# Output projection of a streaming encoder layer: the first norm in two vector steps, and the order of the vector and scalar engines' work around it

## The reference

```
mix = concat([y_a, y_b], -1) @ w_out
x = layer_norm(ALPHA * x + (1 + g1) * mix, ln1_g, ln1_b)
h = layer_norm(x) * (1 + sc2) + sh2
gate, up = split(h @ w_ffn_up, 2)
ffn = (silu(gate) * up) @ w_ffn_down
x = layer_norm(ALPHA * x + (1 + g2) * ffn, ln2_g, ln2_b)
```

## Time and profile before

| | |
|---|---|
| median of 3 runs | 1773.69 us (1767.19, 1773.69, 1774.83) |
| profiled execution, own time | 1767.71 us |
| its span | 1766.1 us |
| busy in the span | PE 1568.9 (89%), DVE 909.8 (52%), ACT 490.5 (28%), POOL 407.5 (23%) |
| mean granted clock of PE | 0.95 of full |

### The profile page before, as it was taken

One profiled execution on the slowest core, in us unless ns is written; L12 is line 12 of the kernel. 1 busy time (PEld: TensorE's weight loads), 2 busy tenths in 40 slices (PEclk: granted clock), 3 DMA queues, 4 the chain that ended last, 5 costly groups with the idle time before them and its releaser, 6 DMA issues.

```text
span 1766.1 us, 25689 instructions
## 1 busy us (share of the span) xinstructions
PE 1568.9 (89%) x9409; PEld 1435.9 (81%) x9409; DVE 909.8 (52%) x1511; ACT 490.5 (28%) x1169; POOL 407.5 (23%) x563
## 2 busy tenths in 40 slices
PE   5897898989886799848879899999999999999994
PEld 3797898979776699737659798998989989899882
DVE  5425566443464467525662545355363462644658
ACT  4531333343443355323443120211202112011110
POOL 4888876600221122113430000000000000000012
PEclk9898999999898899869989999999999999999997
DMA  9221333333333422182115210201202112011112
GB/s 319 74 82 50 97 96 88 105 120 96 114 72 73 123 95 91 7 140 82 71 54 174 71 61 23 59 24 47 71 12 59 42 29 71 23 49 48 28 44 79
DMA packets 139037, 135.25 MB, mean 77 GB/s; under 512 B 14289, under 2 KB 113105, under 8 KB 138961
## 3 DMA queue, kind: packets, MB, share of 16 engines
q1 hardware_dynamic: 135760, 121.48, 24.7%
q10 hardware_dynamic: 2880, 11.72, 1.6%
q0 software_dynamic: 320, 1.05, 0.2%
HBM read 109.54 MB, written 23.51 MB: 75 GB/s over the span
## 4 chain that ended last, share of the span: by engine, by line
PE 43%; DVE 3%; issue 2%; POOL 1%; DMA 1%; ACT 0%; POOLq 0%; DVEq 0%; ACTq 0%; SPq 0%
PE bank L233 29%; PE bank L1681 14%; DMA wraw<-w_up 1%; DVE dtmp L1758 1%; DVE acc L1814 1%; POOL xt L1572 0%; DVE stat L1826 0%; DVE acc L1762 0%; DVE stat L1512 0%; ACT hp L1472 0%; DVE wlo L223 0%; DVE xt L1533 0%; ACT whi L218 0%; POOL rstd L1557 0%; DVE otmp L1530 0%
## 5 line engine op out<-in xcount | busy, mean ns | idle before, releaser
L233 PE MATMUL bank<-hT_hi,whi 128*128 128x384 f32 x1512 | 496.7, 329 | 19.6 <-DVE wlo L223 15.5
L233 PE MATMUL bank<-hT_hi,wlo 128*128 128x384 f32 x1512 | 495.1, 327 | 0.0
L233 PE MATMUL bank<-hT_lo,whi 128*128 128x384 f32 x1512 | 494.8, 327 | 0.0
L233 PEld LDWEIGHTS bank<-hT_hi,whi 128*128 128x128 f32 x1512 | 285.7, 189 | 22.3 <-issue 11.9
L233 PEld LDWEIGHTS bank<-hT_lo,whi 128*128 128x128 f32 x1512 | 285.8, 189 | 0.5
L233 PEld LDWEIGHTS bank<-hT_hi,wlo 128*128 128x128 f32 x1512 | 285.5, 189 | 0.0
L1758 DVE TENSOR_TENSOR dtmp<-bank,g2r 128x512 f32<-128x512 f32 (+1 forms) x198 | 135.3, 686 | 132.6 <-PE bank L1681 132.6
L1663 POOL TENSOR_SCALAR rstd<-stat 128x1 f32<-128x1 f32 (+1 forms) x9 | 11.8, 1313 | 767.6 <-DVE stat L1830 767.6
L1681 PE MATMUL bank<-wd_hi,hid_hi 128*128 128x512 f32 (+1 forms) x396 | 160.4, 405 | 13.7 <-DVE dtmp L1758 13.7
L223 DVE TENSOR_TENSOR wlo<-wraw,whi 128x1024 fp32r<-128x1024 f32 (+1 forms) x73 | 88.8, 1219 | 144.2 <-ACT whi L218 143.9
L1681 PE MATMUL bank<-wd_lo,hid_hi 128*128 128x512 f32 (+1 forms) x396 | 156.4, 395 | 0.0
(11 more groups left out here) (360 smaller groups left out, 2582.9 us busy)
## 6 DMA issues: line engine op xcount, KB each, us to landing
wada<-w_ada SPq DMA_DIRECT2D x12, 2048.0 KB, 14.2
wraw<-w_up SPq DMA_DIRECT2D x44, 512.0 KB, 3.8
wraw<-w_down SPq DMA_DIRECT2D x22, 512.0 KB, 3.5
wraw<-w_in SPq DMA_DIRECT2D x21, 512.0 KB, 4.2
rows<-convrow ACTq DMA_DIRECT2D x16, 577.5 KB, 3.0
stg<-rows SPq DMA_DIRECT2D x9, 768.0 KB, 4.7
xall<-x_prompt SPq DMA_DIRECT2D x8, 512.0 KB, 6.6
wraw<-w_out SPq DMA_DIRECT2D x8, 512.0 KB, 4.1
```

Source lines behind the costliest of these rows:

```text
L233: last = nc.tensor.matmul(ps[banks[c]][:, 0:cw], w[:, slot, k * P:(k + 1) * P], a[:, k, c0:c0 + cw], start=(k == 0 and n == 0), stop=(k == ...
```

## The change

The norm's first application no longer goes through ACT and POOL. DVE itself computes (x - mean) * weight in one instruction and, once POOL has the reciprocal root, * rstd + bias in a second. POOL loses -mean*rstd of the first norm and the addition over the whole tile; ACT loses its first normalising pass. The remainder `wlo` of tile t+2 is made directly behind the first of the two steps, in front of the work on tile t-2. ACT's rounding of `whi` for tile t+2 goes ahead of `modulate`, and ACT, not DVE, rounds the modulated rows to `hT_hi`, behind `modulate`.

```
--- before.py
+++ after.py
@@ -64,7 +64,7 @@
 
 COUNTED_ON = {
     "o_T": ("g_T", 3 * TILES), "wo_mm": ("g_row", TILES), "f_dn": ("g_kv", TILES * HEADS),
-    "ms_hi": ("g_n", 2 * TILES), "o_n1": ("g_kdec", TILES), "o_n2": ("g_E", 3 * TILES), "h2_mod": ("g_so", TILES),
+    "ms_hi": ("g_n", 2 * TILES), "o_n2": ("g_E", 3 * TILES), "h2_mod": ("g_so", TILES),
     "f_hi": ("g_Vb", TILES * HEADS),
     "ms_lo": ("g_mix", TILES), "o_tmp": ("g_S", TILES * HEADS), "o_r": ("g_X", TILES * HEADS * LV), "o_bn": ("g_A", TILES * HEADS),
     "o_mv": ("g_QK", TILES), "o_xg": ("g_qd", TILES), "h2_hi": ("g_Xm", 2 * TILES), "h2_lo": ("g_X0", 2 * TILES),
@@ -1472,6 +1472,8 @@
                     last = act.activation(hp2[:, k, 0:n], ps[6 + k // 4][:, (k % 4) * P:(k % 4) * P + n], ACT.Identity,
                                           scale=onep[:, 1, k, tok:tok + 1], bias=modc[:, 6 + k // 4, k % 4, tok:tok + 1])
                 last.then_inc(on["h2_mod"], 1)
+                act.wait_ge(on["h2_mod"], alone(act, since("h2_mod", u + 1)))
+                act.activation(hT_hi[:, :, tile_cols(u)], hp2[:, :, 0:n], ACT.Copy).then_inc(on["h2_hi"], 1)
 
             def step(t, s):
                 n = tile_rows(t)
@@ -1479,13 +1481,10 @@
                     for j in range(2):
                         act.wait_ge(on["wo_mm"], since("wo_mm", PTILES + j))
                         ffn_hi(act, 0, j)
+                if not (isinstance(t, int) and t > PTILES - 2):
+                    tile_hi(act, t + 2, s)
                 if not (isinstance(t, int) and t < 2):
                     modulate(t - 2)
-                if not (isinstance(t, int) and t > PTILES - 2):
-                    tile_hi(act, t + 2, s)
-                act.wait_ge(on["o_rs"], since("o_rs", t * 2 + 1))
-                act.wait_ge(on["o_bn"], since("o_bn", t * 4 + 2))
-                normalise(act, xt[0:n, s, :], xt[0:n, s, :], n, 0, on["o_n1"])
                 act.wait_ge(on["o_rs"], since("o_rs", t * 2 + 2))
                 act.wait_ge(on["x1_ready"], since("x1_ready", t + 1))
                 act.wait_ge(on["o_T"], since("o_T", t - 1))
@@ -1515,8 +1514,6 @@
 
             def split_h2(u):
                 n = tile_rows(u)
-                dve.wait_ge(on["h2_mod"], since("h2_mod", u + 1))
-                dve.tensor_copy(hT_hi[:, :, tile_cols(u)], hp2[:, :, 0:n]).then_inc(on["h2_hi"], 1)
                 dve.wait_ge(on["h2_hi"], since("h2_hi", u + 1))
                 dve.tensor_tensor(hT_lo[:, :, tile_cols(u)], hp2[:, :, 0:n], hT_hi[:, :, tile_cols(u)].bitcast(F32), ALU.subtract).then_inc(on["h2_lo"], 1)
 
@@ -1537,14 +1534,19 @@
                     for j in range(2):
                         ffn_lo(dve, 0, j)
                 stats(xt[0:n, s, :], n, 0, t * 4 + 2, on["o_mv"])
+                dve.wait_ge(on["ln1_rows"], 32)
+                dve.wait_ge(on["o_mv"], alone(dve, since("o_mv", t * 2 + 1)))
+                dve.scalar_tensor_tensor(out=xt[0:n, s, :], in0=xt[0:n, s, :], scalar=stat[0:n, 0, 12:13], in1=ln1r[0:n, 0, :],
+                                         op0=ALU.subtract, op1=ALU.mult).then_inc(on["o_xg"], 1)
+                if not (isinstance(t, int) and t > PTILES - 2):
+                    tile_lo(dve, t + 2, s)
                 if not (isinstance(t, int) and t < 2):
                     split_h2(t - 2)
-                dve.wait_ge(on["o_n1"], since("o_n1", t + 1))
-                dve.wait_ge(on["ln1_rows"], 32)
-                dve.tensor_tensor(xt[0:n, s, :], xt[0:n, s, :], ln1r[0:n, 0, :], ALU.mult).then_inc(on["o_xg"], 1)
-                if not (isinstance(t, int) and t > PTILES - 2):
-                    tile_lo(dve, t + 2, s)
-                dve.wait_ge(on["x1_ready"], since("x1_ready", t + 1))
+                dve.wait_ge(on["o_rs"], since("o_rs", t * 2 + 1))
+                dve.wait_ge(on["o_xg"], alone(dve, since("o_xg", t + 1)))
+                dve.scalar_tensor_tensor(out=xt[0:n, s, :], in0=xt[0:n, s, :], scalar=rstd[0:n, 0, 0:1], in1=ln1r[0:n, 1, :],
+                                         op0=ALU.mult, op1=ALU.add).then_inc(on["x1_ready"], 1)
+                dve.wait_ge(on["x1_ready"], alone(dve, since("x1_ready", t + 1)))
                 stats(xt[0:n, s, :], n, 1, t * 4 + 4, on["o_mv"])
 
             wo_steps(dve, step)
@@ -1564,12 +1566,11 @@
 
             def step(t, s):
                 n = tile_rows(t)
-                g = Steps(pool, on["o_p"], since("o_p", t * 4))
+                g = Steps(pool, on["o_p"], since("o_p", t * 3))
                 pool.wait_ge(on["o_mv"], alone(pool, since("o_mv", t * 2 + 1)))
-                pool.wait_ge(on["o_n1"], alone(pool, since("o_n1", t)))
-                rstd_steps(pool, g, n, 0, LN_EPS, on["o_rs"])
-                pool.wait_ge(on["o_xg"], alone(pool, since("o_xg", t + 1)))
-                pool.tensor_tensor(xt[0:n, s, :], xt[0:n, s, :], ln1r[0:n, 1, :], ALU.add).then_inc(on["x1_ready"], 1)
+                pool.wait_ge(on["x1_ready"], alone(pool, since("x1_ready", t)))
+                g(pool.tensor_scalar(rstd[0:n, 0, 0:1], stat[0:n, 0, 13:14], LN_EPS, None, ALU.add))
+                pool.tensor_tensor(rstd[0:n, 0, 0:1], rstd[0:n, 0, 0:1], mhalf[0:n, 0:1], ALU.pow).then_inc(on["o_rs"], 1)
                 pool.wait_ge(on["o_mv"], alone(pool, since("o_mv", t * 2 + 2)))
                 pool.wait_ge(on["o_n2"], alone(pool, since("o_n2", t)))
                 rstd_steps(pool, g, n, 1, LN_EPS, on["o_rs"])
```

## The result

| | before | changed |
|---|---|---|
| median, runs of one chip | 1770.87 us (4 runs, 1767.19 to 1774.83) | 1751.53 us (4 runs, 1748.4 to 1753.5) |
| ratio | | 0.9891, 95% interval 0.9868 to 0.9913 |
| span of the profiled execution | 1766.1 us | 1750.0 us |
| PE busy | 1568.9 | 1570.8 |
| DVE / ACT / POOL busy | 909.8 / 490.5 / 407.5 | 919.0 / 488.6 / 387.6 |

What follows compares the result with a forecast made beforehand. A ring of waits through ACT, DVE and POOL was taken to keep PE idle in the output projection. 13.8 + 5.7 + 1.3 - 0.3 = 20.5 us off the 1770.9 mean gives 1750.4 us, range 1744 to 1756.

Steps and rivals of the forecast that it cites:

- The five gaps: Output projection, tiles 4 to 8: PE's five waits for wlo, 10.7 us, all go; tile 8 ends 13.8 us earlier.
- The slack of `wlo`: Output projection: wlo now needs only whi, so DVE can lag by 6 us before PE idles once.
- The ring that stays: Output projection: one turn through ACT, DVE, POOL takes 12.0 us, 13.0 with POOL held; DVE 0.5 late at tile 8.
- POOL under back-to-back vector work: First norm: POOL's two small operations beside DVE's vector instructions cost 0.1 us a tile, between 0 and 1.08.
- Rival 3: Output projection: POOL shut out by three vector instructions, turn 15.1 us, 4.6 us slower, 1775.5 us; chance 0.02.
- Start of the FFN: Behind tile 8: PE's gap before the first FFN weights shrinks from 9.08 to 3.4 us, gaining 5.7 us.
- Clock: First FFN block, 48 matmuls: PE's clock may stay high after the 3.4 us gap, gain 1.3 us, bounds 0 and 2.7.
- Last tile: Before the last hT_lo: ACT rounds at half width instead of DVE's cast, costing 0.3 us.
- Behind it: After the last hT_lo: the next pair's FFN weight loads move along with PE and ACT, costed at nothing.
- Rival 2: Behind the last hT_lo: gain given back by later loads or clock, gain 8 to 14 us, 1757 to 1763; chance 0.08.
- rival 4: In the tiles: PE still waits, whi behind a late xn; 5.4 us gain left, 1765.5 us; chance 0.04.
- Rival 1: Output projection: turn of 13.0 us with POOL held, DVE 4.5 late at tile 8, gain 14.6, 1756 us; chance 0.24.

Runs made afterwards that it cites:

- the two part-alone runs: The changed kernel's norm alone, order and engines of before, ratio 0.9888; the kernel before with whi and wlo early and ACT rounding hT_hi, ratio 1.001.
- the run with the late `hT_lo`: The changed kernel with hT_lo of tile t-2 moved behind the second statistics; ratio to the kernel before 0.9859.
- the early weight: The changed kernel with the first FFN weight split in tile 7's step, a tile earlier; ratio to the kernel before 0.986.
- the filler: The changed kernel with 26 unused matmuls on PE between tile 6's transposes and the first FFN block; ratio to the kernel before 0.9907.

## Why the prediction was right, point by point

*What bounds.* Right: the ring through ACT, DVE and POOL held PE, and the two part-alone runs show it from both sides. The one turn that the prediction read, 15.18, is near the loop's others (14.09, 15.36), but the unrolled tiles ran at 12.96 and 12.51 already.

*The five gaps.* Right. Forecast 13.8 us, measured 13.65 (822.37 to 906.83 is 84.46; 823.79 to 894.60 is 70.81).

*The slack of `wlo`.* True but idle: I gave the moved `wlo` credit for the gaps ("so DVE can lag by 6 us before PE idles once"). With `wlo` back behind `hT_lo` no gap came back either. That order was good enough once the ring was short.

*The ring that stays.* The turn was right (12.0, or 13.0 where POOL is held; measured 12.24, 13.21, 13.31 in the loop). What failed is the step after it, "I take 0.5" for the lag, since at PE's pace DVE would start each tile after a short wait. That holds up to tile 4. But a turn of 12.24 is 0.46 over PE's 11.78; by tile 5 DVE no longer waits for PE, POOL is held behind the residual, and a turn is 13.2. DVE took tile 6 1.8 us late (872.70 for 870.91) and tile 7 2.3 us late (884.99 for 882.69). At tile 8 the shorter unrolled turns had brought it back to 0.9 (895.48 for 894.60), near the 0.5; the lag did its harm one tile earlier, through ACT.

*POOL under back-to-back vector work.* Right in the sum. Rival 3 needed POOL shut out by three vector instructions in a row. In eight of nine tiles each operation was held behind one at most, in tile 5 behind one each: step 1 runs 863.67 to 864.95 and POOL's addition ends 0.09 later; `wlo` runs 864.87 to 866.09 and POOL's power ends 0.43 later. The Trainium skill (SBUF — State Buffer, Who interferes with whom) has whoever issues first keep the shared ports for the whole instruction while the other blocks. In tile 8 the power had to let a second instruction pass, at a cost of 0.46 us of DVE's waiting. The trace agrees with the rule for POOL; it also shows `wlo` starting at its time, 864.87, before the held addition had ended. Nor did DVE pay where POOL came first: in tile 6 the addition started at 876.89, the step at 876.91, and the step took the same 1.28 as in tile 5.

*Start of the FFN.* Mis-sized: forecast 5.7, measured 4.2 (a gap of 4.87 for 9.08). The sentence that failed is "ACT's rounding is early enough, since its second normalisation of tile 7 ends about 0.4 after tile 8". It ended at 898.17, 3.6 after tile 8's matmuls (894.60). Of the 3.2 us between the two, 2.3 are the lag at tile 7; without it the end would still have come 0.9 later than forecast. The rounding of 898.08 stands behind it, and DVE waits 1.22 us for it:

```profile
899.22 1.23 DVE L223 TENSOR_TENSOR wlo<-wraw,whi 128x1024 fp32r<-128x1024 f32 x1 [1.22 <-ACT whi L218]
```

*Clock.* Forecast 1.3 with bounds 0 and 2.7; measured a loss of 0.3: the first block took 11.34 by the chain of waits for 11.01 before (the chain counts it up to some 0.16 us past the start of the transposes, so it is the 11.18 from above). The gap was 4.87, not 3.4, and so above the 3.93 after which it had fallen before. But 3.06 and 3.93 did not enclose a limit, as the prediction took them to: in the run with the late `hT_lo` the clock fell behind a gap of 3.01, and before the change it had already fallen behind one of 2.16, to 0.50 at 868 to 870:

```profile
866.20 0.50 PE L1428 MATMUL bank<-wo_hi,whi 128*128 128x512 f32 x1 [2.16 <-DVE wlo L1452]
```

```profile
868.00:870.00 2.00, 2.00 (x7) 0.50 0.31 125
```

*Last tile.* Forecast a cost of 0.3, measured 0.2 (the gap is 4.12 for 3.93). *Behind it:* nothing that stands out of the scatter of 1.1 us, as forecast. Rival 2 is out by that, rival 4 by the missing gaps in the tiles.

The terms sum to 17.35, not 20.5. The time came out right to 1.1 us (1751.5 for 1750.4) since the medians moved by 19.3, and that closeness is luck in part: the 2 us between those and the stage lie ahead of the stage or in the scatter of the runs; which, the runs don't tell. On the chip where the changed kernel ran again the medians moved by 17.7 (1777.25 to 1759.51). Rival 1 was a third of the way: PE began the FFN 1.6 us later than forecast (900.50 less the 1.42, for 897.5), not 4.5.

## What to carry to other kernels

When an engine idles in each tile, walk its wait back until it closes on itself, and add up one turn: here that turn, and no engine's busy share, was the pace. Taking time out of the ring paid until PE's own 11.78 us a tile was the longer; making an operand early that is not in the ring only moved the wait to the next thing the ring brings. And compare distances between two events of the same stage, not whole times: here one kernel repeated to 0.01 us across the stage in two profiles, while its four runs on one chip spread by 3 to 5.

## What the runs showed of the hardware that was not expected

- The clock after a gap of PE is not a function of the gap alone, as the first blocks of 48 matmuls show, each up to the next transposes' start: gap 2.43 us, 8.43 us long; 3.01, 10.01; 4.87, 11.18; 10.62, 9.84. Before the change a gap of 3.06 had kept the full clock, and a shorter one of 2.16 had lost it. The Trainium skill (TensorE: Matmul & The Clock Gate, What's actually happening) describes a gate between two levels that recent activity opens, and says that the watch on that activity runs freely of the kernel's start, so that one kernel differs between runs. The levels of 0.50 and 1.00 agree with it; filling the gap with useless matmuls brought the 2.7 us back.
- In the changed kernel a POOL operation of 0.57 us takes 1.3 to 1.4 beside a two-input vector instruction, and ends some 0.4 us after it, even when the next such instruction follows at once; in tile 8 it had to let two pass (2.56), in this kernel's second profile and in those of the early weight and of the filler again. What decides which is open.
- The part ahead of the stage, the same code in all kernels, varied most: the output projection's first matmul started between 774.1 and 789.1 us of the span, and between 784.1 and 789.1 in the four kernels profiled on one chip. That, not the stage, is why an edit of 3 us can't be read from whole times.
